# Both score maps of differential attention on TensorE together, on 64 rows each, in two steps by query tile

## What is computed

```
q,k : 8 heads, each with two maps (m = 0, 1) of 64 channels; v, z_a : 8 heads of 128 channels
s[m]  = q[m] @ k[m].T * 64**-0.5, causal                     (512 x 512, per head and map)
a[m]  = softmax(s[m])
p     = a[0] - lam * a[1]
o     = p @ v ;  o = o * rsqrt(mean(o*o) + eps) * gain * (1 - lambda_init)
y_a   = o * z_a * sigmoid(z_a)
```

## Time and profile before

| | |
|---|---|
| median of three runs | 1563.93 us |
| the profiled execution, its own time | 1565.23 us |
| span of its instructions on the core | 1563.5 us |
| PE matmul busy | 1498.8 us (96%) |
| PE weight load busy | 1220.2 us (78%) |
| DVE busy | 819.4 us (52%) |
| ACT busy | 501.1 us (32%) |
| granted PE clock, mean share of full speed | 0.991 |

### The profile page before, as it was taken

How to read it: one execution, slowest core, us unless ns; L and a number is a source line. 1 busy time by engine, 2 the same in 40 slices (tenths; PEclk the granted TensorE clock), 3 DMA queues, 4 the chain that set the end, 5 groups by cost and what they waited for, 6 DMA issues and landing times.

```text
span 1563.5 us, 18079 instructions
## 1 busy us (share of the span) xinstructions
PE 1498.8 (96%) x6600; PEld 1220.2 (78%) x6600; DVE 819.4 (52%) x1072; ACT 501.1 (32%) x693; POOL 44.0 (3%) x52
## 2 busy tenths in 40 slices
PE   2889999999999999999999999999999999999994
PEld 2667788787887878878787888888788888888883
DVE  6997764647546375463754742222522323434448
ACT  1215434425344243443434422223122221422121
POOL 0000000000000000000000000000000000000004
PEclk9999999999999999999999999999999999999997
DMA  9995432533324334233433232322232232362312
GB/s 346 382 382 155 135 108 69 147 107 107 108 85 130 107 111 123 82 114 107 132 110 94 82 135 80 107 93 96 82 107 98 90 107 80 108 254 96 107 54 108
DMA packets 215248, 200.22 MB, mean 128 GB/s; under 512 B 7729, under 2 KB 176433, under 8 KB 214449
## 3 DMA queue, kind: packets, MB, share of 16 engines
q1 hardware_dynamic: 209648, 176.52, 34.9%
q0 software_dynamic: 4608, 16.78, 3.9%
q10 hardware_dynamic: 962, 6.53, 1.0%
HBM read 195.61 MB, written 4.19 MB: 128 GB/s over the span
## 4 chain that ended last, share of the span: by engine, by line
PE 88%; DVE 7%; issue 2%; ACT 1%; DMA 1%; SPq 0%; POOLq 0%; POOL 0%; ACTq 0%; DVEq 0%
PE acc L992 28%; PE acc L993 28%; PE acc L994 28%; DVE mod_sum L631 2%; PE sc L1081 2%; DVE w_lo L604 1%; PE misc L1099 1%; DMA w_mod_in<-in_w_mod 1%; PE sc L1090 1%; DVE res L975 1%; DVE res L951 0%; ACT act_hi L431 0%; DVE gate L653 0%; PE misc L1041 0%; DVE act_lo L658 0%
## 5 line engine op out<-in xcount | busy, mean ns | idle before, releaser
L604 DVE TENSOR_TENSOR w_lo<-raw,w_hi 128x1024 fp32r<-128x1024 f32 (+1 forms) x258 | 310.6, 1215 | 599.6 <-ACT w_hi L388 599.5
L992 PE MATMUL acc<-act_hi,w_hi 128*128 128x512 f32 x1472 | 579.2, 394 | 21.8 <-DVE w_lo L604 13.9
L994 PE MATMUL acc<-act_hi,w_lo 128*128 128x512 f32 x1472 | 574.8, 390 | 0.0
L993 PE MATMUL acc<-act_lo,w_hi 128*128 128x512 f32 x1472 | 574.3, 390 | 0.0
L388 ACT ACTIVATE w_hi<-raw 128x1024 fp32r<-128x1024 f32 (+1 forms) x258 | 268.9, 1052 | 720.0 <-PE acc L994 637.9
L992 PEld LDWEIGHTS acc<-act_hi,w_hi 128*128 128x128 f32 x1472 | 277.2, 188 | 93.6 <-issue 35.8
L994 PEld LDWEIGHTS acc<-act_hi,w_lo 128*128 128x128 f32 x1472 | 277.3, 188 | 58.6
L993 PEld LDWEIGHTS acc<-act_lo,w_hi 128*128 128x128 f32 x1472 | 277.5, 189 | 56.7 <-issue 0.2
L994 PE MATMUL acc<-y_hi,w_lo 128*128 128x512 f32 x256 | 99.6, 389 | 0.0
L992 PE MATMUL acc<-y_hi,w_hi 128*128 128x512 f32 x256 | 99.6, 389 | 0.0
L993 PE MATMUL acc<-y_lo,w_hi 128*128 128x512 f32 x256 | 99.6, 389 | 0.0
(11 more groups left out here) (151 smaller groups left out, 990.9 us busy)
## 6 DMA issues: line engine op xcount, KB each, us to landing
raw<-in_w_in SPq DMA_DIRECT2D x256, 256.0 KB
w_mod_in<-in_w_mod SPq DMA_DIRECT2D x64, 512.0 KB, 6.9
raw<-in_w_tail SPq DMA_DIRECT2D x32, 1024.0 KB
raw<-in_w_in SPq DMA_DIRECT2D x29, 1024.0 KB
gate_in<-in_w_mod POOLq DMA_DIRECT2D x32, 512.0 KB, 4.2
x_in<-in_xT SPq DMA_DIRECT2D x8, 512.0 KB, 8.0
x_tok<-in_x ACTq DMA_DIRECT2D x1, 4096.0 KB, 13.2
raw<-in_w_in SPq DMA_DIRECT2D x8, 384.0 KB
```

The lines of the kernel that those rows point to most:

```text
L604: ins = dve.tensor_tensor(w_lo[:, f % SLOTS, :, 0:width], raw[:, (f // 2) % 2, 2 * (f % 2):2 * (f % 2) + 2, 0:width], w_hi[:, f % SLOTS, : ...
L992: pe.matmul(dst, a_hi, b_hi, start=first, stop=False)
L993: pe.matmul(dst, a_hi, b_lo, start=False, stop=False)
L994: return pe.matmul(dst, a_lo, b_hi, start=False, stop=last)
```

## The change

The score products are regrouped. Step 0 (PE at s = 1, DVE and ACT at s = 2) has query tiles 3 and 2 of both maps, step 1 (s = 3, s = 4) has tiles 1 and 0 of both maps. Within a step the maps alternate: tile 3 of map 0, tile 3 of map 1, tile 2 of map 0, tile 2 of map 1. Neighbouring products thus use different halves of the partitions, and their outputs lie in different banks. Step 0 needs four full banks, so map 1 of tile 2 goes to `misc`. For that reason the transposes of v move behind the scores of s = 3, and ACT's copy to `v_tok` moves from the start of s = 2 to the end of s = 4. The sigmoid of z_a moves on DVE from the end of `rotate` to s = 6. `row_max` gets 8 columns. The number of products, transposes, masks, maxima and exponentials is the same.

```diff
+PHASE_TILES = ((3, 2), (1, 0))
+SCORE_AT = {(0, 3): (0, 0), (0, 2): (1, 0), (1, 3): (2, 0), (1, 2): (3, 0),
+            (0, 1): (0, 0), (0, 0): (0, 256), (1, 1): (1, 0), (1, 0): (1, 256)}
+TURNED_AT = {3: (0, 0), 2: (1, 0), 0: (1, 384), 1: (2, 0)}
+        def scores(m, t, first, last):
+            b, c0 = SCORE_AT[m, t]
+            return misc[:, c0 + first:c0 + last] if b == 3 else sc[:, b, c0 + first:c0 + last]
...
@@ ACT attend_and_convolve
-                if s == 2:
+                if s in (2, 4):
+                    phase = (s - 2) // 2
+                    act.wait_ge(max_ready, i * 2 + (phase + 1))
+                    act.wait_ge(p_ready, i + BASE)
+                    act.wait_ge(p_turned, i + BASE)
+                    for m, prob in enumerate((prob0, prob1)):
+                        for t in PHASE_TILES[phase]:
+                            w = (t + 1) * P
+                            e = act.activation(prob[:, PROB_AT[t]:PROB_AT[t] + w], scores(m, t, 0, w),
...
+                    e.then_inc(exp_done, 1)
+                if s == 4:
                     act.wait_ge(v_turned, i + 1 + BASE)
                     act.wait_ge(o_done, i + BASE)
                     copy(v_tok[:, :], misc[:, :]).then_inc(v_ready, 1)
...
@@ DVE rotate: the last six lines go to attend_and_convolve
+                if s == 6:
+                    dve.wait_ge(bank_drained[3], i * 2 + 1 + BASE)
+                    own(dve.tensor_scalar(e_a[:, :], e_a[:, :], 1.0, None, ALU.add))
+                    settle_hc()
+                    own(dve.reciprocal(e_a[:, :], e_a[:, :]))
+                    settle_hc()
+                    own(dve.tensor_tensor(z_a[:, :], z_a[:, :], e_a[:, :], ALU.mult))
...
@@ DVE attend_and_convolve
+                    both = [(m, t) for m in range(2) for t in PHASE_TILES[phase]]
+                    dve.wait_ge(scores_done, i * 2 + (phase + 1 + BASE))
+                    for m, t in both:
+                        edge = scores(m, t, t * P, (t + 1) * P)
...
@@ PE attend
                 if s == 1:
-                    pe.wait_ge(bank_drained[2], i * 2 + 1 + BASE)
                     pe.wait_ge(o_drained, i + BASE)
-                    for t in range(NT):
-                        ins = pe.transpose(misc[:, t * P:(t + 1) * P], v_f[:, t * P:(t + 1) * P], ident)
-                    ins.then_inc(v_turned, 1)
...
                 if s in (1, 3):
-                    m = (s - 1) // 2
-                    rows = slice(m * DH, (m + 1) * DH)
+                    for t in PHASE_TILES[(s - 1) // 2]:
+                        for m in range(2):
+                            rows = slice(m * DH, (m + 1) * DH)
+                            ins = pe.matmul(scores(m, t, 0, (t + 1) * P), q_f[rows, t * P:(t + 1) * P],
+                                            k_f[rows, 0:(t + 1) * P], start=True, stop=True)
+                    ins.then_inc(scores_done, 1)
+                if s == 3:
+                    pe.wait_ge(bank_drained[2], i * 2 + 1 + BASE)
                     for t in range(NT):
...
+                        ins = pe.transpose(misc[:, t * P:(t + 1) * P], v_f[:, t * P:(t + 1) * P], ident)
+                    ins.then_inc(v_turned, 1)
```

More of the change, by code:

```diff
@@ L76 @@
 HALVES = O0 + (D // COLS) * OUT_HALVES
-SCORE_AT = {3: (0, 0), 2: (1, 0), 0: (1, 384), 1: (2, 0)}
+PHASE_TILES = ((3, 2), (1, 0))
+SCORE_AT = {(0, 3): (0, 0), (0, 2): (1, 0), (1, 3): (2, 0), (1, 2): (3, 0),
+            (0, 1): (0, 0), (0, 0): (0, 256), (1, 1): (1, 0), (1, 0): (1, 256)}
+TURNED_AT = {3: (0, 0), 2: (1, 0), 0: (1, 384), 1: (2, 0)}
 PROB_AT = {3: 0, 2: 512, 0: 896, 1: 1024}
@@ L122, in decoder_block @@
         neg_lam = sb("neg_lam", [P, 1])
-        row_max = sb("row_max", [P, 4])
+        row_max = sb("row_max", [P, 8])
         neg_max = sb("neg_max", [P, 8])
@@ L454, in attend_and_convolve @@
             def attend_and_convolve(i, s):
-                if s == 2:
+                if s in (2, 4):
[7 more added lines that the diff above has]
+                            e = act.activation(prob[:, PROB_AT[t]:PROB_AT[t] + w], scores(m, t, 0, w),
+                                               ACT.Exp, bias=neg_max[:, 4 * m + t:4 * m + t + 1],
+                                               scale=DH ** -0.5,
+                                               accum_out=row_sum[:, 4 * m + t:4 * m + t + 1])
+                    e.then_inc(exp_done, 1)
+                if s == 4:
                     act.wait_ge(v_turned, i + 1 + BASE)
@@ L460, in attend_and_convolve @@
                     copy(v_tok[:, :], misc[:, :]).then_inc(v_ready, 1)
[L461 to L474, removed]
                 if s == 6:
@@ L744, in rotate @@
                     dve.tensor_tensor(dst[:, :], plain[:, :], turned[:, :], ALU.add).then_inc(qk_ready, 1)
[L746 to L751, removed]
             def attend_and_convolve(i, s, settle_hc, base):
@@ L764, in attend_and_convolve @@
                 if s in (2, 4):
-                    m = (s - 2) // 2
-                    dve.wait_ge(scores_done, i * 2 + (m + 1 + BASE))
-                    for t in range(NT):
-                        b, c0 = SCORE_AT[t]
-                        edge = sc[:, b, c0 + t * P:c0 + (t + 1) * P]
+                    phase = (s - 2) // 2
+                    both = [(m, t) for m in range(2) for t in PHASE_TILES[phase]]
+                    dve.wait_ge(scores_done, i * 2 + (phase + 1 + BASE))
+                    for m, t in both:
+                        edge = scores(m, t, t * P, (t + 1) * P)
                         ins = dve.tensor_tensor(edge, edge, mask, ALU.min)
@@ L773, in attend_and_convolve @@
                     settle_hc()
[L774 to L777, removed]
+                    for m, t in both:
+                        ins = dve.tensor_reduce(row_max[:, 4 * m + t:4 * m + t + 1],
+                                                scores(m, t, 0, (t + 1) * P), AX.X, ALU.max)
                     own(ins)
                     settle_hc()
-                    dve.tensor_scalar(neg_max[:, 4 * m:4 * m + 4], row_max[:, :], -DH ** -0.5, None,
-                                      ALU.mult).then_inc(max_ready, 1)
+                    pairs = slice(2, 4) if phase == 0 else slice(0, 2)
+                    dve.tensor_scalar(neg_max[:, :].rearrange("p (m t) -> p m t", m=2)[:, :, pairs],
+                                      row_max[:, :].rearrange("p (m t) -> p m t", m=2)[:, :, pairs],
+                                      -DH ** -0.5, None, ALU.mult).then_inc(max_ready, 1)
                 if s == 4:
@@ L1087, in attend @@
                     for j in range(NT):
-                        b, c0 = SCORE_AT[3 - j]
+                        b, c0 = TURNED_AT[3 - j]
                         for t in range(j, NT):
```

## The result

The changed kernel takes 1546.41 us (median of four runs, 1545.09 to 1547.35), the kernel before 1563.98 (four runs): ratio 0.9885, 95% interval 0.9873 to 0.9898, faster by 17.6 us. I had said 1553.5, and 1549.5 to 1565.0 as the range. The direction was right; the size lies outside the range, on the far side of it.

The account below looks back on a forecast made before the run. PE was taken to bound the kernel; 8 heads x 1.29 us of overlap, called 10.4 us with head 0, off the median 1563.9 gave 1553.5 us, other parts 0 on the path; range 1549.5 to 1565.

Parts of the forecast that it names:

- What bounds the kernel: In the loop over heads PE is never idle, so each microsecond saved on scores counts 8 times.
- Cost of the edges: Entering and leaving the 64-row form drains 0.09 to 0.10 us each; as many edges as before, so zero change.
- Part 1: PE's score passes: alternating halves of the rows overlap, saving 1.29 us a head, 10.3 us in all.
- best bound: Score passes starting in program order, overlapping on different rows: step 0 takes 1.93 us; 1.51 us a head saved, 12.1 in all.
- The second bound: Same order of score passes, with a 0.11 us load exposed at each change of rows: 1.07 a head saved, 8.6 in all.
- Own queues for both halves: Rival: both maps' score passes run wholly beside each other, saving 2.16 us a head, 17.3 in all; 1546.6 us; chance 0.08.
- rival 1: Score passes on different rows run in sequence, no overlap and no cost: 1563.9 us, no change; chance 0.17.
- rival 2: Each change of rows between score passes drains and reloads, 9.6 us lost: 1573.5 us; chance 0.08.
- Part 2: Transposes of v moved from s = 1 to s = 3 on PE: 0.44 us a head before and after, together 0.
- Part 3: Sigmoid of z_a moved on DVE to s = 6: masks of s = 2 some 4.0 us earlier, 4.45 fits into 5.42 idle.
- Part 4: Uneven steps on DVE and ACT: step 0's exponentials ready with slack at least 1.9 us, 0 on the path.
- cover: Part 3's moved sigmoid, not felt by PE itself, makes room on DVE for part 4's longer step 0.

Follow-up runs that it names:

- uneven pairs: Changed kernel with widths crossed between alternating maps (step 0: 512 of map 0, 384 of map 1, 384 of map 0, 512 of map 1): 1547.14 us.
- six ahead: Changed kernel with tiles 3, 2, 0 in step 0, all map 0 products before map 1's: 1554.03 us; with map 0's short ones first 1549.39 us.
- four ahead: Changed kernel with tiles 3, 2, 0 in step 0, four passes of map 0 before map 1's first: 1547.65 us.

## Why the prediction was wrong, point by point

- **What bounds the kernel: right.** Every microsecond of score passes saved on PE came through: 2.17 a head, 17.4 by the periods, 17.6 by the medians.
- **Cost of the edges: right.** The number of changes between 64-row and 128-row form is the same, and so was their cost: the saving of 2.17 leaves 0.01 for all edges together beside the 2.16 of the streams.
- **Part 1, the overlap of the two halves: the step that failed.** "A1, then A2 beside B1, B2 beside C1": I took one list of passes in program order, with map 0's second pass ahead of map 1's first, and called the result the best bound. It wasn't a bound. Each half works off its own passes, as long as no more than four passes of the other half stand ahead in the program. Step 0 lasted 1.51 us, where this list gave 1.93. The term was put at 1.29 us a head, with 1.51 as the most; it measured 2.17. The second bound, with loads exposed at each change of rows, rested on "a weight load starts only when the pass ahead of it has started"; that holds within one half, and no row of before has both halves at work.
- **The rivals.** Own queues for both halves was written down with its working, 2.16 a head and 1546.6 us, and the measurement is 1546.4. What it assumes, that the halves never wait for each other, holds only within the limit of four passes, which this kernel stays inside. I gave it 0.08 and left it out of the range, on the ground that "a second pass of A stands ahead of B". No row of before stood behind this ground; it was the only thing said against the rival. With no row for either side, a range that ended at a bound from an assumed order was too narrow. The run with both maps on the same rows is rival 1's time, 1563.7, and nothing like rival 2's drain at each change of rows was seen.
- **Part 2, the transposes of v: right at 0.** Their piece of the chain reads 0.59 instead of 0.44, since they now come right behind the 64-row form and the change of form is counted with them; the large product behind the scores of step 1 no longer carries it. For head 0 I had put 0.18 us for scores that wait for the rotary of k. The load path stood idle for 0.51 us ahead of their first load, against 0.35 in head 1, so it cost 0.16:

```profile
168.50 0.18 PEld L1087 LDWEIGHTS sc<-prob_t 64*128 64x128 f32 x1 [0.51 <-DVE prob_t L753]
```

- **Part 3, the sigmoid: right.** It begins behind `w_lo` at s = 6 and leaves 0.96 us of idle time ahead of the next one, where I had 0.97:

```profile
290.77 3.35 DVE L807 RECIPROCAL e_a<-e_a 128x512 f32<-128x512 f32 x1
...
295.81 1.23 DVE L613 TENSOR_TENSOR w_lo<-raw,w_hi 128x1024 fp32r<-128x1024 f32 x1 [0.96 <-ACT w_hi L397]
```

- **Part 4, slack: right, and now priced.** The last exponential of step 0 ends thus:

```profile
272.56 0.21 ACT L475 ACTIVATION_READ_ACCUMULATOR prob<-misc,neg_max 128x1 f32 x1
```

at 272.8, and PE wants it 2.7 us later (its next group starts its load at 275.59, 0.1 behind the end of the half); I had said at least 1.9. PE's matmuls waited for no engine in the loop. What I called cover, without a price, is worth 11.6 us.

## What to carry to other kernels

Where PE is the bound, float32 products with a contraction of 64 can be laid on both halves of the rows, into different banks. The pair then costs what one costs, loads included, as long as no more than four passes of one half stand ahead of the other half's next pass in the program. Within that limit the order is free and may serve other ends. One thing wants care: the semaphore that reports the scores hangs on the last product in the program. In the run with uneven pairs the last pass of that product started at 264.74, ahead of the other half's last one at 264.52 + 0.32 = 264.84. There both ended level (264.74 + 0.43 = 265.17 and 264.84 + 0.32 = 265.16); whether one such signal is enough when one half has more to do wasn't tried. Where no row shows a mechanism, bound it by the work of one unit alone, not by an order of starts that is only assumed; and when a step is made longer for an engine behind, look at once for what can leave that engine's queue ahead of it.

## What the runs showed of the hardware

- Two float32 products on partitions 0 to 63 and 64 to 127 start within 0.02 us of each other and take no longer than one alone (0.43 us for 512 columns), and so do their weight loads.
- Both halves can leave program order: a pass of 512 columns that is later in the program started 0.21 us ahead of one of 384 on the other half.
- The other half can pass over four passes, not six. It was held while four earlier passes were unstarted, and started within 0.01 us of the moment when three were, in both runs that had six ahead; in the run with four, the load of map 1's second product did the same. Every product here is two passes with a load each, so whether passes, whole products or passes with their loads are counted wasn't told apart.
